# Two heads at a time in the banded and the forgetting attention of a two-block transformer kernel

## The reference

```
fcum = cumsum(log_sigmoid(z_forget + bias))              # 8 heads x 512 tokens
s = q @ k.T / 8 + fcum[query] - fcum[key]                # causal
o_f = softmax(s) @ v
# banded: s = q @ k.T / 8 in a window of 128, softmax over (s, sink), times v
y = (concat(o_d, o_f) * silu(z_gate)) @ w_out
```

## Time and profile before

| | us |
|---|---|
| median of 3 runs | 2313.68 (2312.69 to 2314.06) |
| the profiled execution | 2314.38 |
| its span, first to last instruction | 2312.6 |
| mean granted TensorE clock | 0.948 of 2.4 GHz |
| banded attention with what is woven in | 134 to 262 |
| differential attention | 509 to 605 |
| forgetting attention with what is woven in | 614 to 763 |

### The profile page before, as it was taken

The page is one execution under the profiler, slowest core; times in us unless marked ns, Lnnn a source line. Parts: engine busy times, 40 slices in busy tenths (PEclk is TensorE's granted clock), DMA queues, the critical chain, the costliest instruction groups (busy, mean ns, idle before and its releaser), DMA issues.

```text
span 2312.6 us, 26804 instructions
## 1 busy us (share of the span) xinstructions
PE 2168.9 (94%) x9974; PEld 1687.4 (73%) x9974; DVE 1481.3 (64%) x2635; ACT 925.5 (40%) x1737; POOL 13.9 (1%) x15
## 2 busy tenths in 40 slices
PE   4898998999899989988999999899999989999998
PEld 2665566776665776757788887688888867888886
DVE  6566665666345569976655655799999965433333
ACT  3334444344333343333332333566665643232231
POOL 1000000000000000000000000000000000000000
PEclk8998999899889979988999999899999999999999
DMA  7431212233212411103555554111111112333331
GB/s 306 164 110 59 81 59 79 100 119 128 91 55 92 145 38 46 55 0 137 202 179 183 195 178 146 46 55 56 46 53 57 48 38 64 108 96 95 96 95 55
DMA packets 65983, 228.75 MB, mean 99 GB/s; under 512 B 7104, under 2 KB 9280, under 8 KB 65728
## 3 DMA queue, kind: packets, MB, share of 16 engines
q1 hardware_dynamic: 65856, 227.05, 29.0%
HBM read 224.93 MB, written 2.10 MB: 98 GB/s over the span
## 4 chain that ended last, share of the span: by engine, by line
PE 76%; DVE 14%; DMA 3%; ACT 3%; issue 3%; SPq 0%; DVEq 0%; ACTq 0%
PE bank L377 20%; PE bank L379 19%; PE bank L378 19%; DVE arena L1553 5%; PE bank L1815 5%; DMA w_raw<-weights_dram 3%; PE bank L1005 3%; PE bank L1028 3%; PE bank L673 2%; DVE w_lo L315 1%; PE bank L1016 1%; DVE ada_raw L510 1%; DVE arena L494 1%; PE bank L1852 1%; PE bank L698 1%
## 5 line engine op out<-in xcount | busy, mean ns | idle before, releaser
L377 PE MATMUL bank<-h_hi,w_hi 128*128 128x512 f32 (+1 forms) x1616 | 673.9, 417 | 35.1 <-DVE h_lo L640 14.5
L379 PE MATMUL bank<-h_hi,w_lo 128*128 128x512 f32 (+1 forms) x1616 | 644.2, 399 | 0.0
L378 PE MATMUL bank<-h_lo,w_hi 128*128 128x512 f32 (+1 forms) x1616 | 643.2, 398 | 0.0
L306 ACT ACTIVATE w_hi<-w_raw 128x1024 fp32r<-128x1024 f32 (+3 forms) x293 | 291.5, 996 | 416.6 <-DMA w_raw<-weights_dram 242.1
L315 DVE TENSOR_TENSOR w_lo<-w_raw,w_hi 128x1024 fp32r<-128x1024 f32 (+3 forms) x290 | 333.1, 1149 | 181.3 <-ACT w_hi L306 181.0
L377 PEld LDWEIGHTS bank<-h_hi,w_hi 128*128 128x128 f32 (+1 forms) x1616 | 311.7, 193 | 116.8 <-issue 49.1
L379 PEld LDWEIGHTS bank<-h_hi,w_lo 128*128 128x128 f32 (+1 forms) x1616 | 310.7, 192 | 70.4 <-issue 0.3
L378 PEld LDWEIGHTS bank<-h_lo,w_hi 128*128 128x128 f32 (+1 forms) x1616 | 312.1, 193 | 63.3 <-issue 4.7
L377 PE MATMUL bank<-a_hi_t,w_hi 128*128 128x512 f32 x512 | 203.1, 397 | 1.4 <-DVE a_lo_t L1481 1.4
L378 PE MATMUL bank<-a_lo_t,w_hi 128*128 128x512 f32 x512 | 203.0, 396 | 0.0
L379 PE MATMUL bank<-a_hi_t,w_lo 128*128 128x512 f32 x512 | 202.9, 396 | 0.0
(11 more groups left out here) (239 smaller groups left out, 2517.1 us busy)
## 6 DMA issues: line engine op xcount, KB each, us to landing
w_raw<-weights_dram SPq DMA_DIRECT2D x261, 512.0 KB, 4.2
ada_raw<-ada_dram SPq DMA_DIRECT2D x128, 512.0 KB, 3.6
arena<-ada_dram SPq DMA_DIRECT2D x8, 1024.0 KB, 15.7
w_raw<-weights_dram SPq DMA_DIRECT2D x16, 256.0 KB, 2.8
xT<-x_dram SPq DMA_DIRECT2D x1, 2048.0 KB, 14.4
out_dram<-xT SPq DMA_DIRECT2D x8, 256.0 KB, 2.2
tables<-tables_dram SPq DMA_DIRECT2D x1, 1536.0 KB, 19.8
w_raw<-weights_dram SPq DMA_DIRECT2D x8, 144.0 KB, 3.5
```

The lines of the kernel that those rows point to most:

```text
L306: nc.scalar.activation(WH[:, slot, 0:w], RAW[:, raw, 0:w], ACT.Copy).then_inc(w_hi_ready, 1)
L377: nc.tensor.matmul(o, WH[:, slot, cols], self.hi(k), start=(k == 0), stop=False)
L378: nc.tensor.matmul(o, WH[:, slot, cols], self.lo(k), start=False, stop=False)
L379: last = nc.tensor.matmul(o, WL[:, slot, cols], self.hi(k), start=False, stop=(k == self.K - 1))
```

## The change

A new class `PairAttention` takes the place of `Attention` in `swa` and `fox`; the other two attentions stay. A unit is now a pair of heads and a block of queries, 16 units, and a unit takes two steps. TensorE at an even step s = 2u: the sums of unit u-2 (both heads, for each block of keys first the even head into partitions 0 to 63 of bank 7, then the odd head into 64 to 127), the scores of unit u (both heads one behind the other, banks 4 and 5; the forgetting attention's two mask matmuls follow), the transposes of the even head of unit u-1. At an odd step: the transposes of the odd head of unit u-1. ScalarE at an even step: exponential of the even head of unit u, copy of the even head's transposes of unit u-1, exponential of the odd head; at an odd step the copy of the odd head's transposes. VectorE at an even step: the two maxima of unit u; at an odd one the product with the gates where a pair of heads is complete, and the two heads' weights. The buffers keep their number: four rows of weights, two transposed rows, now one for each head. ForgetRows' steps 2 to 7 move from the places 6.1, 10.1, ... 26.1 to 6.2, 6.9, 14.2, 14.9, 22.2, 22.9.

```diff
+        class PairAttention(Stage):
...
+                self.units = [(g, i) for g in range(len(heads) // 2) for i in range(NT)]
+                U = len(self.units)
+                self.steps = 2 * U + 4
+                self.scored, self.max_ready = signal("scored").take(2 * U), signal("max_ready").take(2 * U)
+                self.exp_ready, self.p_ready = signal("exp_ready").take(2 * U), signal("p_ready").take(2 * U)
+                self.turned, self.pt_ready = signal("turned").take(2 * U), signal("pt_ready").take(2 * U)
+                self.out_done = signal("out_done").take(U)
...
+            def row_read(self, h):
+
+                return self.max_ready.sem, self.max_ready.at(2 * NT * (h // 2 + 1) - 1 + h % 2)
+
+            def pe_step(self, pe, s):
+                U, u = len(self.units), s // 2
+                if s == 0:
+                    for m, k in self.ready:
+                        pe.wait_ge(m.sem, m.at(k))
+                    for b in (4, 5, 6, 7):
+                        free_bank(pe, self.before[b])
+                if s % 2 == 0 and 2 <= u < U + 2:
+                    self.pe_sums(pe, u - 2)
+                if s % 2 == 0 and u < U:
+                    self.pe_scores(pe, u)
+                if 1 <= u < U + 1:
+                    self.pe_turn(pe, u - 1, s % 2)
+
+            def pe_scores(self, pe, u):
+                g, i = self.units[u]
+                js = self.keys(i)
+                w = P * len(js)
+                k0 = js[0] * P
+                if i == 0:
+                    for m in self.made.get(g, ()):
+                        pe.wait_ge(m.sem, m.at(1))
+                if u:
+                    pe.wait_ge(self.max_ready.sem, self.max_ready.at(2 * u))
+                for m in range(2):
+                    q, k = self.heads[2 * g + m][0]
+                    last = nc.tensor.matmul(bank[4 + m][:, 0:w], q[:, i * P:(i + 1) * P], k[:, k0:k0 + w], start=True, stop=self.forget is None)
+                    if self.forget is None:
+                        last.then_inc(self.scored.sem, 1)
+                if self.forget is not None:
+                    for m in range(2):
+                        nc.tensor.matmul(bank[4 + m][:, w - P:w], bm_ident, bm_causal, start=False, stop=True).then_inc(self.scored.sem, 1)
+
+            def pe_turn(self, pe, v, m):
+                r = 2 * v + m
+                n = len(self.keys(self.units[v][1]))
+                pe.wait_ge(self.p_ready.sem, self.p_ready.at(r + 1))
+                if r:
+                    pe.wait_ge(self.pt_ready.sem, self.pt_ready.at(r))
+                for a in range(n):
+                    last = nc.tensor.transpose(bank[6][:, a * P:(a + 1) * P], self.E[r % 4][:, a * P:(a + 1) * P], ident)
+                last.then_inc(self.turned.sem, 1)
+
+            def pe_sums(self, pe, v):
+                g, i = self.units[v]
+                js = self.keys(i)
+                pe.wait_ge(self.pt_ready.sem, self.pt_ready.at(2 * v + 2))
+                if g and i == 0:
+                    pe.wait_ge(self.out_read.sem, self.out_read.at(g))
+                for a, j in enumerate(js):
+                    for m in range(2):
+                        last = nc.tensor.matmul(bank[7][64 * m:64 * m + 64, i * P:(i + 1) * P], self.heads[2 * g + m][1](j), self.PT[m][:, a * P:(a + 1) * P],
+                                                start=(a == 0), stop=(a == len(js) - 1), skip_group_check=True)
+                last.then_inc(self.out_done.sem, 1)
...
+            def act_step(self, act, s):
+                U, u = len(self.units), s // 2
+                if s % 2 == 0 and u < U:
+                    self.act_exp(act, u, 0)
+                if 1 <= u < U + 1:
+                    self.act_copy(act, u - 1, s % 2)
+                if s % 2 == 0 and u < U:
+                    self.act_exp(act, u, 1)
+
+            def act_exp(self, act, u, m):
+                g, i = self.units[u]
+                r = 2 * u + m
+                e = self.E[r % 4][:, 0:P * len(self.keys(i))]
+                act.wait_ge(self.max_ready.sem, self.max_ready.at(r + 1))
...
+            def act_copy(self, act, v, m):
+                n = len(self.keys(self.units[v][1]))
+                act.wait_ge(self.turned.sem, self.turned.at(2 * v + m + 1))
+                if v:
+                    act.wait_ge(self.out_done.sem, self.out_done.at(v))
+                nc.scalar.activation(self.PT[m][:, 0:n * P], bank[6][:, 0:n * P], ACT.Copy).then_inc(self.pt_ready.sem, 1)
...
+                if s % 2 == 0:
+                    if u < U:
+                        self.dve_max(dve, u)
+                    return
+                done = u >= 2 and self.units[u - 2][1] == NT - 1
+                if done:
+                    g = self.units[u - 2][0]
+                    dve.wait_ge(self.out_done.sem, self.out_done.at(u - 1))
+                    self.finish.take(dve, g, self.out_read)
+                if u < U:
+                    self.dve_weights(dve, u)
+                if done and self.finish.split:
+                    self.finish.split(dve, g)
+
+            def dve_max(self, dve, u):
+                g, i = self.units[u]
+                w = P * len(self.keys(i))
+                for m in range(2):
+                    r, h = 2 * u + m, 2 * g + m
...
+                    dve.wait_ge(self.scored.sem, self.scored.at(r + 1))
+                    if r >= 4:
+                        dve.wait_ge(self.turned.sem, self.turned.at(r - 3))
+                        dve.wait_ge(self.exp_ready.sem, self.exp_ready.at(r - 3))
...
+                    nc.vector.tensor_tensor_reduce(self.E[r % 4][:, 0:w], bank[4 + m][:, 0:w], added, -self.scale, lowest, ALU.add, ALU.min,
+                                                   STAT[:, 8 + r % 4:9 + r % 4]).then_inc(self.max_ready.sem, 1)
...
+            def dve_weights(self, dve, u):
+                w = P * len(self.keys(self.units[u][1]))
+                for m in range(2):
+                    r = 2 * u + m
+                    e = self.E[r % 4][:, 0:w]
+                    dve.wait_ge(self.exp_ready.sem, self.exp_ready.at(r + 1))
...
+                    dve_done(nc.vector.reciprocal(ri, sm))
+                    dve.wait_ge(dve_done.sem, dve_done.n)
+                    nc.vector.tensor_scalar(e, e, ri, None, ALU.mult).then_inc(self.p_ready.sem, 1)
...
             def act_step(self, act, h):
                 act.wait_ge(self.done.sem, self.done.at(h + 1))
                 if h >= 2:
-                    act.wait_ge(self.scores.max_ready.sem, self.scores.max_ready.at(NT * (h - 1)))
+                    act.wait_ge(*self.scores.row_read(h - 2))
...
-            swa = Attention([([(Z[64 * (h % 2):64 * (h % 2) + 64, SQ + h // 2, :], Z[64 * (h % 2):64 * (h % 2) + 64, SV - h // 4, :])],
-                              (lambda j, h=h: VS[:, j, 64 * (h // 4):64 * (h // 4) + 64])) for h in range(8)], 64.0 ** -0.5,
-                            swa_out, [late(r) for r in range(4)], [late(4), late(5)], ready=[(keys.copied, 3)], window=True, sink=True,
-                            made={2 * g: (after(r2.roped, 1 + g),) for g in range(4)})
+            swa = PairAttention([((Z[64 * (h % 2):64 * (h % 2) + 64, SQ + h // 2, :], Z[64 * (h % 2):64 * (h % 2) + 64, SV - h // 4, :]),
+                                  (lambda j, h=h: VS[:, j, 64 * (h // 4):64 * (h // 4) + 64])) for h in range(8)], 64.0 ** -0.5,
+                                swa_out, [late(r) for r in range(4)], [late(4), late(5)], ready=[(keys.copied, 3)], window=True, sink=True,
+                                made={g: (after(r2.roped, 1 + g),) for g in range(4)})
...
-            fox = Attention([([(Z[64 * (h % 2):64 * (h % 2) + 64, FQ + h // 2, :], Z[64 * (h % 2):64 * (h % 2) + 64, FK + h // 2, :])],
-                              (lambda j, h=h: FVT[:, j, 64 * h:64 * h + 64])) for h in range(8)], 64.0 ** -0.5,
-                            fox_out, E, PT, ready=[(diff.out_read, 4)], forget=rows,
-                            made={2 * g: (after(a2.free, g), after(a2.free, 4 + g), after(tf.copied, g)) for g in range(4)})
+            fox = PairAttention([((Z[64 * (h % 2):64 * (h % 2) + 64, FQ + h // 2, :], Z[64 * (h % 2):64 * (h % 2) + 64, FK + h // 2, :]),
+                                  (lambda j, h=h: FVT[:, j, 64 * h:64 * h + 64])) for h in range(8)], 64.0 ** -0.5,
+                                fox_out, E, PT, ready=[(diff.out_read, 4)], forget=rows,
+                                made={g: (after(a2.free, g), after(a2.free, 4 + g), after(tf.copied, g)) for g in range(4)})
...
-            weave((rows, -2, 0.1, 0, 2), (rows, 6.1, 4, 2, 8), (fox, 0, 1), (gates, 0.2, 0.85), (hn, 2.4, 1, 0, 4), (hn, 6.4, 1, 4, 5), (hn, 8.4, 1, 5, 9), (hn, 29.4, 1, 9, 13))
```

(1 more changed line is left out.)

33 lines of the change are left out of this document (added).

## The result

The median of five runs is 2275.59 us (2271.11 to 2277.22) against 2314.06 us (2312.69 to 2319.4): a ratio of 0.9827, 95% interval 0.9811 to 0.9842, about 40 us or 1.7% faster. The profiled execution took 2276.38 us (span 2274.6), 38.0 us of span less than before. The forecast was 2290, and the range ended at 2278: the direction was right and the size too small.

A forecast was written before the change was run, and what follows sets the result against it. TensorE, busy 94% of the span, was taken as the bound. 14.3 + 15.9 - 1.3 - 1.0 - 2.5 - 2.7 + 3.0 - 2.0 = 23.7 us gained; 2314.4 - 23.7 - 0.7 = 2290 us, range 2278 to 2306.

The forecast's parts named there:

- The overlap: Both changed attention stages: two heads' scores, and two heads' sums, cost what one head's cost; 14.3 us banded, 15.9 forgetting middle.
- first rival: Sums in both stages: columns do not overlap, so the sums' 14.2 us stay; 2304 us, chance 15%.
- The transposes ... keep their number: Both changed stages: the number of transposes stays as before; no saving was counted for them.
- (d): First forgetting steps, head norm's sums waiting for ScalarE's square: 3.7 us lost, about 4.2 saved, counted as 0.
- (a): A pair's second transposes wait for ScalarE's copy behind the next pair's exponential: 1.3 us lost in forgetting middle, 1.0 banded.
- (b): VectorE's work for each gate tile comes at once, delaying maxima or weights: 2.5 us lost, both stages, between 0 and 6.
- (f): New waits may bring the low clock to matmuls: 2.0 us lost, 10 matmuls at 0.2, between 0 and 10.
- (c): Forgetting stage: forget rows come two behind one another, the second product waits for ScalarE's copy: 3 times 0.9, 2.7 us lost.
- (e): Sums of a new pair of heads no longer wait 1.63 us for the output to be read: 3.0 us gained.
- third rival: Forgetting middle: new short waits leave PE at 1.2 GHz; 70 us if throughout, 35 for half, 2325 us; chance 5%.
- One sign of being wrong: The prediction called itself wrong if the waits before transposes came to more than 10 us.
- second rival: The lock step eats the gain: waits at second transposes 1 us larger in 25 pairs, 25 us; 2315 us, chance 7%.

The follow-up runs named there:

- twelfth run: Changed kernel with the even head's sums ahead of the pair's scores and the odd head's behind them: 2283.97 us, 0.9871 against the kernel before.
- fourth run: Changed kernel with the even step's old order, scores, transposes, sums, in place of sums, scores, transposes: 2281.55 us, 0.9854 against the kernel before.
- tenth run: Kernel before the change, with the modulation tiles' DMAs issued by GpSimd in place of SyncE: 2295.95 us, 0.9923 against the kernel before.
- third run: Changed kernel with a pair's sums issued head by head in place of block by block: 2283.25 us, 0.9864 against the kernel before.

## Why the prediction was right in direction and short in size

**The overlap** stood, for scores and for sums. The prices of two and four blocks came out to 0.02 us, and the first rival, that columns do not overlap, is refuted by the 0.59 and 1.02 us and by the twelfth run. Scores and sums gave 16.0 us in the forgetting stage's middle against 15.9.

What made the forecast short are two terms that I put at nothing, the transposes and the start of the forgetting stage.

**"The transposes ... keep their number"**, and I priced them as unchanged. This is the first step that failed. The number stayed, the price did not: 7.7 us less over both stages (4.6 banded, 2.7 in the middle, 1.2 at the start, 0.8 more at the end). I had taken 0.37 us for two from the earlier trace rows, a distance to a group of another form, and did not see that the new order puts gates behind them. The fourth run shows that what follows a group makes its price. By the table the saving is 7.7 us; no run shows how much of it reached the time.

**(d), "I count 0"**, is the second. The stretch gave 7.8 us. The walk to the waits was near: 2.25, 0.88, 2.50 and 0 us against 2.5, 0.9, 2.9 and 1.0. But against it I set four groups, 4.2 us, where scores and sums gave 5.9, and nothing for the transposes (1.2) or for a clock that came back sooner: gates 1.7 less, 23 of them at the low clock and not 29. The idle time rose by 2.0, not 3.7. How much of the 7.8 belongs to the forgetting stage's new code stays open: the old code took 38.7 and 38.6 us in the kernel before, 35.2 in the tenth run and 32.5 behind the new banded stage; the new code took 30.9, and 30.1 behind the old banded stage, but 33.2 in the third run, which changes next to nothing there. What sets the clock at that start I did not find.

**The banded stage** came out at 14.0 us, near the sum that I gave it, but by two errors against each other. Scores and sums gave 19.0 us instead of 14.3, since the stretch that VectorE sets and the last sums were shortened too, and transposes another 4.6; the idle time rose by 9.0, and terms (a), (b) and (f) had foreseen about 3 us of loss for this stage. How far the two errors cancelled was luck. The 3.50 us behind a late tile of weights is the largest single one. That VectorE sets the stretch from 212 us was right: after, 203 to 219 us, it is busy for 13.7 of 15.9 us and TensorE for 7.5.

**(a) and (c)**, the waits behind the copies, exist where I put them, in the middle of the forgetting stage: 4.9 us of idle time in all, the longest 1.85, against 1.3 + 2.7 and a part of (b) and (f), 6.2 us. In the banded stage term (a) was far too small: outside the stretch that VectorE sets, TensorE waited 6.8 us before transposes where I had 1.0, half of it behind the late tile. **(e)**, the wait of the earlier trace rows for the output to be read, is gone from that place; one of 0.63 us for the same cause stands at 231.36 us. **The end** gave 1.0 us where I had 0.

**The clock.** The third rival is refuted: the middle's granted clock is 1.00, with a transpose group in every step. The Trainium skill's rule ("TensorE: Matmul & The Clock Gate", Part 4), that transposes do not count as busy, had no effect that the rows here show.

**One sign of being wrong came true.** I had named waits before transposes of more than 10 us. TensorE waited 19.4 us before transposes in the two stages, where it had waited 7.8: 11.6 us more. The second rival, that the lock step eats the gain, is still refuted as it was priced: in the stretches that count the waits before transposes are 9.1 us, not 25, and the time fell. But its direction was right: these waits were longer than my terms, and gains that I had not counted covered them.

In sum the span fell by 14 us more than forecast: some 8 from transposes and nearly 7 from the start of the forgetting stage without them, with small terms of both signs beside. My range had "some microseconds in the stretches I gave nothing" and reached to 36 us. The start of the forgetting stage and the transposes, a term I had not listed, gave together more than that.

## What to carry to other kernels

Price a group of matmuls by the distance to the next group only together with what follows it: if a change alters the follower, the price changes, here by 0.1 to 0.2 us for each transpose group. Two heads' products in two halves of TensorE cost what one costs when they are issued alternately with nothing of full size between; head by head that held for two blocks and no longer for three. When a busy engine gives up 54 us of work in two stages, expect a part of it back as waits (20 us here), and look at what a waiting instruction stands behind, one engine further back: a DMA issue queued behind another's wait cost this kernel, before as after, 16 to 18 us.

## What the runs showed of the hardware beyond what I expected

- Column halves of TensorE overlap in fp32 at no cost when alternated (1.02 us for two heads of four blocks, 1.01 for one), and in part when not: 1.51 us for head after head, by estimate about two products of the second head running beside the first's.
- One full-height bf16 product between two row halves takes the whole overlap away: 0.63 + 0.16 + 0.63 us in place of 0.63.
- A group of transposes costs more ahead of these sums than ahead of gates (0.37 and 0.19 us for two, 0.53 and 0.35 for four). Ahead of whole-array sums it costs 0.27 and 0.49, so the width of the follower explains only a part.
- The start of the forgetting stage, much of it at the low clock, took 38.7 and 38.6 us in two executions of one kernel, and 35.2 and 32.5 us with the same code of that stage in two other kernels, each profiled once. The cause is open.
